# The MLP's up projection on 512 and 128 token columns in place of twice 320

## The reference

```
x = x + rms_norm(mix, p['norm_mix_post'])
hn = rms_norm(x, p['norm_mlp_pre'])
u = jnp.square(jax.nn.relu(hn @ p['w_up'])) @ p['w_down']
x = x + rms_norm(u, p['norm_mlp_post'])
```

## Time and profile before

| | |
|---|---|
| Time, median of 3 runs (lowest to highest) | 1650.34 us (1649.36 to 1650.79) |
| Profiled execution, first to last instruction (span) | 1646.9 us |
| Profiled execution, its own time | not given; the span stands 3.4 us below the median |
| Busy: TensorE, VectorE, ScalarE, GpSimd | 96%, 43%, 37%, 2% of the span |
| DMA over the span | 143.40 MB, mean 87 GB/s |
| Mean granted TensorE clock | 0.986 |

### The profile page before, as it was taken

How to read it: one execution, slowest core, us unless ns; L and a number is a source line. 1 busy time by engine, 2 the same in 40 slices (tenths; PEclk the granted TensorE clock), 3 DMA queues, 4 the chain that set the end, 5 groups by cost and what they waited for, 6 DMA issues and landing times.

```text
span 1646.9 us, 27655 instructions
## 1 busy us (share of the span) xinstructions
PE 1583.6 (96%) x10590; PEld 1530.0 (93%) x10590; DVE 701.0 (43%) x1202; ACT 616.0 (37%) x1100; POOL 25.5 (2%) x31
## 2 busy tenths in 40 slices
PE   7999999989999999999999999998799999999996
PEld 6999999989999989998988999998699999999996
DVE  7444454442248773334544542341633333232334
ACT  6222322222237772234454542133551341431522
POOL 1000000000000000000000000000200000000001
PEclk9999999999999999999999999999799999999999
DMA  4645444412222322231431422432022222222221
GB/s 136 153 126 136 130 116 116 129 52 68 76 71 58 86 67 65 74 96 53 119 93 51 118 67 77 143 100 64 26 76 77 70 80 68 75 76 77 76 78 64
DMA packets 255669, 143.40 MB, mean 87 GB/s; under 512 B 7654, under 2 KB 252071, under 8 KB 255612
## 3 DMA queue, kind: packets, MB, share of 16 engines
q1 hardware_dynamic: 255620, 142.72, 30.7%
HBM read 129.86 MB, written 12.84 MB: 87 GB/s over the span
## 4 chain that ended last, share of the span: by engine, by line
PE 85%; DVE 7%; ACT 4%; issue 3%; DMA 1%; DVEq 0%; ACTq 0%; POOL 0%; SPq 0%
PE psum L540 72%; PE psum L674 2%; PE psum L638 2%; PE psum L806 1%; PE psum L643 1%; DVE arena L1404 1%; PE psum L669 1%; PE psum L849 1%; DVE arena L1644 1%; ACT arena L1171 1%; PE psum L654 1%; DVE arena L1792 1%; PE psum L606 1%; PE psum L617 1%; PE psum L844 1%
## 5 line engine op out<-in xcount | busy, mean ns | idle before, releaser
L540 PE MATMUL psum<-XH,w_hi 128*128 128x320 f32 x1936 | 610.8, 315 | 3.8 <-ACT arena L1161 1.8
L540 PE MATMUL psum<-XH,w_lo 128*128 128x320 f32 x1936 | 600.2, 310 | 0.0
L540 PE MATMUL psum<-XL,w_hi 128*128 128x320 f32 x1936 | 599.9, 310 | 0.0
L540 PEld LDWEIGHTS psum<-XH,w_hi 128*128 128x128 f32 x1936 | 365.5, 189 | 11.8 <-DVE w_lo L1386 5.3
L540 PEld LDWEIGHTS psum<-XL,w_hi 128*128 128x128 f32 x1936 | 365.5, 189 | 0.8
L540 PEld LDWEIGHTS psum<-XH,w_lo 128*128 128x128 f32 x1936 | 365.1, 189 | 0.0
L1386 DVE TENSOR_TENSOR w_lo<-w_raw,w_hi 128x1024 fp32r<-128x1024 f32 x185 | 226.3, 1223 | 299.1 <-ACT w_hi L1001 298.4
L540 PE MATMUL psum<-YH,w_hi 128*128 128x320 f32 x1024 | 318.2, 311 | 3.0 <-DVE YL L1777 2.0
L1001 ACT CAST w_hi<-w_raw 128x1024 fp32r<-128x1024 f32 x185 | 193.4, 1046 | 335.0 <-PE psum L540 305.7
L540 PE MATMUL psum<-YL,w_hi 128*128 128x320 f32 x1024 | 317.6, 310 | 0.0
L540 PE MATMUL psum<-YH,w_lo 128*128 128x320 f32 x1024 | 317.4, 310 | 0.0
(11 more groups left out here) (226 smaller groups left out, 1282.3 us busy)
## 6 DMA issues: line engine op xcount, KB each, us to landing
w_raw<-in_w_in_dram SPq DMA_DIRECT2D x88, 512.0 KB, 3.7
w_raw<-in_w_up_dram SPq DMA_DIRECT2D x32, 512.0 KB, 4.0
w_raw<-in_w_down_dram SPq DMA_DIRECT2D x32, 512.0 KB, 3.8
w_raw<-in_w_branch_dram SPq DMA_DIRECT2D x24, 512.0 KB, 3.9
arena<-in_cache_fox_k_dram SPq DMA_DIRECT2D x8, 1024.0 KB
arena<-in_cache_fox_v_dram SPq DMA_DIRECT2D x8, 1024.0 KB
out_dram<-arena SPq DMA_DIRECT2D x16, 256.0 KB, 2.5
arena<-in_state_gla_dram SPq DMA_DIRECT2D x4, 1024.0 KB, 5.4
```

The source lines that it names most:

```text
L540: mm = pe.matmul(Z[h][:, 0:HT], w[s][:, k, :], x[:, k, h * HT:(h + 1) * HT], start=(k == 0 and i == 0), stop=(k == KT - 1 and i == 2))
```

## The change

The up projection gets a matmul loop of its own, `up`, in TensorE's `group`. It moves the tokens as columns 0 to 511 (prompt) and 512 to 639 (samples), each still in its own bank. Order, operands and number of the matmuls are as before, 48 per block. ScalarE's `up` and VectorE's subtraction use the same two parts. The wait ahead of the MLP asks for 2 x `NT` + 2 x `NTP` = 18 pieces, where it asked for 16. The down projection and all other projections keep twice 320.

```diff
+        UP = (slice(0, TP), slice(TP, T))
...
-            pe.wait_ge(nt_free, 2 * NT + 2 * (HT // P + 1))
+            pe.wait_ge(nt_free, 2 * NT + 2 * NTP)
...
                 b = g * (2 * KT) + B_MLP
-                pairs(b, KT // 2, XH, XL, lambda h, k: pe.wait_ge(nt_free, 4 * NT) if (h, k) == (1, 0) else None)
+
+                def up(b, s):
+
+                    pe.wait_ge(w_lo, (b + 1).v)
+                    for h, part in enumerate(UP):
+                        pe.wait_ge(z_free[h], b.v)
+                        if h == 1:
+                            pe.wait_ge(nt_free, 4 * NT)
+                        for k in range(KT):
+                            for i, (w, x) in enumerate(((WH, XH), (WH, XL), (WL, XH))):
+                                mm = pe.matmul(Z[h][:, 0:part.stop - part.start], w[s][:, k, :], x[:, k, part],
+                                               start=(k == 0 and i == 0), stop=(k == KT - 1 and i == 2))
+                        mm.then_inc(z_done[h], 1)
+
+                with pe.Fori(0, KT // 2) as i:
+                    for s in range(2):
+                        up(b.loop(2, i) + s, (b.c + s) % 2)
...
             def up(b, j, n):
-                for h in range(2):
-                    half = slice(h * HT, (h + 1) * HT)
+                for h, half in enumerate(UP):
                     act.wait_ge(z_done[h], (b + 1).v)
                     act.wait_ge(u_done[h], (n + 1).v)
-                    act.activation(UR[:, half], Z[h][:, 0:HT], ACT.Relu).then_inc(z_free[h], 1)
+                    act.activation(UR[:, half], Z[h][:, 0:half.stop - half.start], ACT.Relu).then_inc(z_free[h], 1)
...
-                        for h in range(2):
-                            half = slice(h * HT, (h + 1) * HT)
+                        for h, half in enumerate(UP):
                             dve.wait_ge(u_hi, (up_hi.loop(4, i) + (2 * s + h + 1)).v)
```

## The result

| | before | after |
|---|---|---|
| Time, median of 4 runs (lowest to highest) | 1650.14 us (1649.36 to 1650.79) | 1686.12 us (1685.7 to 1687.61) |
| Ratio, 95% interval | | 1.0218 (1.0204 to 1.0233) |
| Profiled execution | span 1646.9 us | 1685.84 us, span 1684.1 us |

The account below looks back on a forecast made before the run. TensorE's matmul count times interval bounds the MLP, with the weight load as floor for narrow matmuls. Pairs cost 226.7 + 111.6 against 293.4 ns; 768 pairs add 34.5 us to 1650.3, giving 1684.8 us, range 1649 to 1700.

Parts of the forecast that it names:

- The bound: MLP on TensorE: nothing waits; its time is the number of matmuls times their interval, 3072 at 146.7 ns.
- The wide matmul: Up projection, 768 matmuls of 512 columns: 226.7 ns each, ends 215.6 and 234.7.
- the excess of 13.4 ns: Line 540's matmuls: part of the 146.7 ns interval above the 133.3 ns streaming of 320 columns, taken as unchanged at 512.
- The narrow matmul: Up projection, 768 matmuls of 128 columns: the weight load decides, 111.6 ns each, ends 105 and 123.4.
- the linear 66.7: Narrow up matmul's cost in ns if the interval were linear in its columns, 53.3 + 13.4; not taken.
- The sum: Up projection: 338.3 against 293.4 ns per pair, 44.9 more; 768 pairs make 34.5 us, ends 20.9 and 49.7.
- The eviction and the waits: Eviction on ScalarE and VectorE, and the wait raised from 16 to 18 pieces before the MLP: both claimed to cost nothing.
- The short load: Rival, narrow up matmul: fp32r weights load in a quarter of the ticks, narrow costs 66.7 ns; 1650.3 us, chance 0.08.
- The faster rival: Up projection: excess belongs to the 320-column form; wide 215.6, narrow 55.6 ns, 17 us less, 1633.3 us; chance 0.05.
- The dearer ones: Narrow up matmuls: whole 189 ns load between them, four ticks a column, or falling clock; 1744.3 or 1770.5 us; chance 0.09.

Follow-up runs that it names:

- wide and narrow in turn: Changed kernel (512 and 128 columns), each narrow matmul following the wide one with the same weights, up blocks on two pairs of banks: 1689.62 us, ratio 1.0239.
- at 448: Up projection split into 448 and 192 columns, against the kernel before: 1667.04 us, ratio 1.0104.
- the half load: Changed kernel, 512 and 128 columns, but the narrow matmul loads and uses only 64 of 128 output features: 1648.91 us, ratio 0.9992 to the kernel before.
- The wait alone: Kernel before, 320 + 320, with only the wait ahead of the MLP changed from 16 to 18 pieces: 1650.72 us, ratio 1.0003.
- 384 + 256: Up projection split into 384 and 256 columns, against the kernel before: 1649.57 us, ratio 0.9999.
- at 320 columns half a load: 320 + 320 in the changed kernel's loop, every up matmul loading only 64 of 128 output features: 1649.67 us, ratio 0.9998 to the kernel before.

## Why the prediction was right

*The bound.* That TensorE waits for nothing but its own loads in the MLP, and that its time is the number of matmuls times their interval, held in nearly every run: after the first group, which starts at the granted clock of 0.50, each kernel's groups follow from their two intervals to within 0.1 us per block. The one exception is the 0.24 us at the turn to the down blocks with wide and narrow in turn.

*The wide matmul.* Forecast 226.7 ns between 215.6 and 234.7, measured 226 over the ten intervals shown. Taking the excess of 13.4 ns as fixed was right for 384 (173.5 against 173.4) and 512 columns; at 448 it is 3 ns short.

*The narrow matmul.* Forecast 111.6 from line 674, measured 111.4. The choice of the row with the same load, and not of the linear 66.7, carried the whole forecast, and the half load shows that the reason given was the right one. Line 674 alone could not have shown it, since its own stream is as long as the load. One sentence of the prediction is too strong: that no interval can be shorter than a load. A single one can, where the load was fetched under a longer matmul: 0.05 us after the first narrow matmul of a block the next one starts. But that one then waits, so in a row of narrow matmuls, and over a pair, the floor holds.

*The sum.* 34.5 us were forecast, 36.5 are in the chain. The missing 2 us are a term that the sum did not have: a block takes 65.36 / 8 = 8.170 us, its 48 steady intervals 24 x (226.7 + 111.4) = 8.114, and 0.056 x 32 blocks is 1.8 us. They lie at the head of the block. The rest is in the four down groups, 56.38 us where those behind 320 + 320 up blocks take 56.32: their first matmul waits for a load that the narrow matmul ahead is too short to hide.

*The eviction and the waits.* Costed at nothing, and nothing it was. In the block shown, whose last wide matmul ends the first part at about 1191.8, relu of that part is done at 1192.58, 1.7 us before the bank's next matmul at 1194.29, and its subtraction at 1194.87, 3.0 us after the last wide matmul where 3.3 were estimated; the narrow part is done at 1195.99. The wait alone changed nothing. The timeline of ScalarE and VectorE for that block:

```profile
1191.98 0.60 ACT L1374 ACTIVATE arena<-psum 128x512 f32<-128x512 f32 x1 [3.67 <-PE psum L911]
...
1194.18 0.69 DVE L1839 TENSOR_TENSOR YL<-arena,YH 128x512 f32 x1 [4.61 <-ACT YH L1377]
...
1195.70 0.29 DVE L1839 TENSOR_TENSOR YL<-arena,YH 128x128 f32 x1 [0.83 <-ACT YH L1377]
```

*The rivals.* The short load fell with the 111.4 ns and the half load together: fp32r weights take about 108 ns for 128 columns. The Trainium skill, "TensorE: Matmul & The Clock Gate", section "Weight-path perf modes", has fast weight load on for 128 weights of any type but FP32; by this trace fp32r does not count as another type. The same page of the Trainium skill, section "LDWEIGHTS (loading the stationary operand)", gives columns / 1.2 ns, by which 128 columns take an estimated 107 ns; the trace agrees, 111.4 as an interval and 54 for the 64 columns saved. The faster rival fell with the wide matmul, which kept its excess. The dearer ones asked for 189 ns and more between narrow matmuls and fell with the 111.4, and the granted clock stayed at 1.00 in the narrow stretch (busy times of that stretch, in the columns of the earlier trace rows):

```profile
1191.70:1194.30 2.60, 2.60 (x26) 2.60 (x24) 0.12 (x1) 1.85 (x3) 0.00 (x0) 1.00 0.51 152
```

No complete version tried beats the kernel before; 384 + 256 equals it.

## What to carry to other kernels

When tokens are split into unequal parts under the same weights, the price of a part is the larger of its own matmul time and one weight load, and a long part did not lend its slack to a short one in either of the two orders tried. So look in the trace for the time from the first load after an idle TensorE to the second: that is the floor of the interval in a row of matmuls, 0.11 us here, which 256 columns cover and 192 do not. In these runs a split into two parts cost nothing while both stayed above it.

## What the runs showed of the hardware that was not expected

The time above streaming is neither a constant nor a part of the load. It was 12.7 to 13.5 ns at 256, 320, 384 and 512 columns, about 16 at 448 (203 against 186.7), and 6.7 at 128 columns once the load was out of the way (60 against 53.3); at 320 columns half a load left it as it was, and at the granted clock of 0.50 it is absent at 320 columns. What it is stays open.

The first wide matmuls of a block take 0.23 to 0.24 us instead of 0.226, 56 ns per block in all, in up and down blocks alike once both are 512 columns wide. It shows at 512 columns alone: at 448 the intervals are even from a block's second matmul on, and with 320 columns a down block's 7.048 us are 48 x 146.7 to within 6 ns. It is there without square, cast and subtraction, and in a block at whose head no relu runs; whether it comes from the waits at the head of the block or from somewhere else was not tried, and the cause stays open.
